# Five tiles instead of two sum the residual and the last expert's product in PSUM, at the end of a hybrid decoder layer

## The reference

```python
out = jnp.zeros_like(t)
for e in range(N_EXPERTS):
    a = t @ p['w_gate'][e]
    u = t @ p['w_up'][e]
    out = out + combine[:, e:e + 1] * ((jax.nn.silu(a) * u) @ p['w_down'][e])
...
x = x + mix @ p['w_out']
x = x + _moe(_rmsnorm(x, p['norm2_g']), p)
...
y = xf * lax.rsqrt(jnp.mean(xf * xf, axis=-1, keepdims=True) + EPS) * g
```

## Time and profile before

| | us |
|---|---|
| median of three runs | 755.19 |
| lowest, highest | 754.53, 789.18 |
| span of the profiled execution, first to last instruction | 752.6 |
| PE busy in it | 664.4 (88%) |
| DVE busy | 273.3 (36%) |
| ACT busy | 161.3 (21%) |

### The profile page before, as it was taken

The page is one execution under the profiler, slowest core; times in us unless marked ns, Lnnn a source line. Parts: engine busy times, 40 slices in busy tenths (PEclk is TensorE's granted clock), DMA queues, the critical chain, the costliest instruction groups (busy, mean ns, idle before and its releaser), DMA issues.

```text
span 752.6 us, 9463 instructions
## 1 busy us (share of the span) xinstructions
PE 664.4 (88%) x3280; PEld 320.5 (43%) x3280; DVE 273.3 (36%) x546; ACT 161.3 (21%) x317; POOL 89.3 (12%) x161
## 2 busy tenths in 40 slices
PE   8999989999998999986999997877787877779995
PEld 4488878863556333332333332322232322223331
DVE  7798995295366221120111111111111111112057
ACT  3677411321613011110111110101001001001033
POOL 5100000000001111211022121112111111111000
PEclk9999999999999999997999999999989999999998
DMA  9523006469556999999999999999999999999993
GB/s 328 202 112 113 1 13 267 177 259 432 190 196 229 363 412 404 409 378 396 425 417 396 402 415 395 420 402 408 410 391 391 422 412 410 402 391 413 425 356 119
DMA packets 29574, 246.55 MB, mean 328 GB/s; under 512 B 6578, under 2 KB 7090, under 8 KB 16592
## 3 DMA queue, kind: packets, MB, share of 16 engines
q1 hardware_dynamic: 22784, 233.95, 77.4%
q0 software_dynamic: 5280, 8.20, 3.3%
q10 hardware_dynamic: 1456, 3.62, 1.3%
HBM read 235.65 MB, written 19.20 MB: 339 GB/s over the span
## 4 chain that ended last, share of the span: by engine, by line
PE 47%; DMA 34%; DVE 11%; ACT 2%; issue 2%; another core or an unknown queue 1%; SPq 1%; POOLq 0%; DVEq 0%
PE psA L1389 25%; PE psB L1389 22%; DMA mem<-in_w_gu 19%; DMA mem<-in_w_down 11%; DVE mem L710 5%; DMA mem<-y_d 2%; DVE mem L934 1%; DMA mem<-in_w_vb 1%; DMA y_d<-mem 1%; ACT front_c L643 1%; DVE mem L849 1%; PE psA L1394 1%; ACT mem L651 1%; DVE mem L861 1%
## 5 line engine op out<-in xcount | busy, mean ns | idle before, releaser
L1389 PE MATMUL psA<-mem 128*64 128x512 f32 (+7 forms) x1348 | 317.4, 535 | 31.7 <-DMA mem<-in_w_gu 15.7
L1389 PE MATMUL psB<-mem 128*64 128x512 f32 (+7 forms) x1210 | 274.0, 552 | 34.7 <-DMA mem<-in_w_gu 17.8
L1389 PEld LDWEIGHTS psA<-mem 128*64 128x64 f32 (+4 forms) x1348 | 145.0, 154 | 184.4 <-issue 142.1
L1389 PEld LDWEIGHTS psB<-mem 128*64 128x64 f32 (+3 forms) x1210 | 110.9, 154 | 178.0 <-issue 132.7
L710 DVE TENSOR_TENSOR mem<-mem 128x512 f32<-128x512 f32 (+17 forms) x116 | 67.3, 595 | 23.8 <-ACT mem L543 19.6
L1307 POOL DMA_INDIRECT y_d<-front_c,mem x30 | 27.5, 916 | 288.8 <-DVE front_c L1114 288.8
L1142 DVE TENSOR_TENSOR front_c<-front_c,psB 64x512 f32<-64x512 f32 x15 | 10.3, 690 | 125.6 <-ACT front_c L643 125.6
L1142 DVE TENSOR_TENSOR front_c<-front_c,psA 64x512 f32<-64x512 f32 x15 | 10.3, 690 | 119.3 <-ACT front_c L643 119.3
L1302 POOL DMA_INDIRECT mem<-hn_d,mem x34 | 33.4, 984 | 92.6 <-DMA hn_d<-front_c 65.0
L643 ACT ACTIVATE front_c<-psA 64x512 f32<-64x512 f32 x15 | 8.8, 588 | 120.3 <-PE psA L1389 120.3
L643 ACT ACTIVATE front_c<-psB 64x512 f32<-64x512 f32 x15 | 8.8, 588 | 120.1 <-PE psB L1389 120.1
(11 more groups left out here) (244 smaller groups left out, 391.4 us busy)
## 6 DMA issues: line engine op xcount, KB each, us to landing
mem<-in_w_gu SPq DMA_DIRECT2D x64, 2048.0 KB, 38.9
mem<-in_w_down SPq DMA_DIRECT2D x32, 2048.0 KB, 44.3
mem<-in_w_out SPq DMA_DIRECT2D x2, 2048.0 KB, 7.9
y_d<-mem SPq DMA_DIRECT2D x1, 4096.0 KB, 11.8
mem<-y_d SPq DMA_DIRECT2D x8, 512.0 KB, 8.4
mem<-in_x_T SPq DMA_DIRECT2D x8, 260.0 KB, 8.6
mem<-in_w_vb SPq DMA_DIRECT2D x8, 256.0 KB, 8.8
mem<-in_x_prompt SPq DMA_DIRECT2D x4, 512.0 KB, 11.1
```

The costliest lines, as they stand in the source:

```text
L1389: return nc.tensor.matmul(out, lhsT, rhs, start=start, stop=stop, skip_group_check=True)
```

## The change

All five tiles are now summed in PSUM. PE multiplies the identity with `x2` for tiles 4, 2 and 3 too, after their `kept`; for the tile of 8 rows the identity is cut to 8 x 8. `add_kept`, its three sums on DVE and the semaphore `f_sum` are gone. ACT waits for `f_ps` in every tile and squares from PSUM. DVE scales all tiles from PSUM. The order of the tiles and their banks stay.

```diff
-        IN_PSUM = (0, 1)
...
             for n, t in enumerate(LAST_ORDER):
                 r = ROWS[t]
-                if t in IN_PSUM:
-                    act.wait_ge(f_ps, n + 1)
-                    total = LAST_PS[t]
-                else:
-                    act.wait_ge(f_sum, n + 1 - len(IN_PSUM))
-                    total = x2[0:r, t, :].rearrange("p (a n) -> p a n", a=2)
-                A(yin[...], total, ACT.Square, accum_out=fx[0:r, t:t + 1]).then_inc(f_sq, 1)
+                act.wait_ge(f_ps, n + 1)
+                A(yin[...], LAST_PS[t], ACT.Square, accum_out=fx[0:r, t:t + 1]).then_inc(f_sq, 1)
...
-            def add_kept(n, t):
-                dve.wait_ge(f_ps, n + 1)
-                dve.wait_ge(f_acc, n + 1)
-                x2t = x2[0:ROWS[t], t, :].rearrange("p (a n) -> p a n", a=2)
-                tt(x2t, x2t, LAST_PS[t], ALU.add).then_inc(f_sum, 1)
...
-            for n in range(2):
-                scaled(n, n)
-            add_kept(2, LAST_ORDER[2])
-            for n in range(3, NT):
-                add_kept(n, LAST_ORDER[n])
-                scaled(n - 1, LAST_ORDER[n - 1])
-            scaled(NT - 1, LAST_ORDER[NT - 1])
+            for n, t in enumerate(LAST_ORDER):
+                scaled(n, t)
...
-            rest(0)
-            pe.wait_ge(y_last, 2)
-            kept(0, 0)
-            rest(1)
-            kept(1, 1)
-            kept(2, LAST_ORDER[2])
-            kept(3, LAST_ORDER[3])
-            pe.wait_ge(f_done, 1)
-            kept(4, LAST_ORDER[4])
+            rest(0, 0, True)
+            pe.wait_ge(y_last, 2)
+            kept(0, False).then_inc(f_ps, 1)
+            rest(1, 1, True)
+            kept(1, False).then_inc(f_ps, 1)
+            for n in (2, 3):
+                kept(LAST_ORDER[n], True)
+                rest(n, LAST_ORDER[n], False).then_inc(f_ps, 1)
+            pe.wait_ge(f_done, 1)
+            kept(LAST_ORDER[4], True)
+            rest(4, LAST_ORDER[4], False).then_inc(f_ps, 1)
```

More of the change, by code:

```diff
@@ L262, in build @@
             sem, "x2_out zero_out tokens_rdy cw3_rdy cw_ps picks_rdy rest_out y_last".split())
-        f_acc, f_ps, f_sum, f_sq, f_rt, f_done, f_out = map(sem, "f_acc f_ps f_sum f_sq f_rt f_done f_out".split())
+        f_acc, f_ps, f_sq, f_rt, f_done, f_out = map(sem, "f_acc f_ps f_sq f_rt f_done f_out".split())
         block = ctx.enter_context(nc.Block())
@@ L686, in _ @@
                 r = ROWS[t]
-                if t in IN_PSUM:
-                    act.wait_ge(f_ps, n + 1)
-                    total = LAST_PS[t]
-                else:
-                    act.wait_ge(f_sum, n + 1 - len(IN_PSUM))
-                    total = x2[0:r, t, :].rearrange("p (a n) -> p a n", a=2)
-                A(yin[0:r, 2 * t, :].rearrange("p (a n) -> p a n", a=2), total, ACT.Square, accum_out=fx[0:r, t:t + 1]).then_inc(f_sq, 1)
+                act.wait_ge(f_ps, n + 1)
+                A(yin[0:r, 2 * t, :].rearrange("p (a n) -> p a n", a=2), LAST_PS[t], ACT.Square, accum_out=fx[0:r, t:t + 1]).then_inc(f_sq, 1)
                 act.wait_ge(f_sq, n + 1)
@@ L1211, in _ @@
                 add_rows(t)
-            def add_kept(n, t):
-                dve.wait_ge(f_ps, n + 1)
-                dve.wait_ge(f_acc, n + 1)
-                x2t = x2[0:ROWS[t], t, :].rearrange("p (a n) -> p a n", a=2)
-                tt(x2t, x2t, LAST_PS[t], ALU.add).then_inc(f_sum, 1)
             def scaled(n, t):
                 r = ROWS[t]
-                total = LAST_PS[t] if t in IN_PSUM else x2[0:r, t, :].rearrange("p (a n) -> p a n", a=2)
                 dve.wait_ge(f_rt, n + 1)
                 link(V.reciprocal(ss[0:r, 3, t:t + 1], ss[0:r, 2, t:t + 1]))
-                V.scalar_tensor_tensor(x2[0:r, t, :].rearrange("p (a n) -> p a n", a=2), total, ss[0:r, 3, t:t + 1],
+                V.scalar_tensor_tensor(x2[0:r, t, :].rearrange("p (a n) -> p a n", a=2), LAST_PS[t], ss[0:r, 3, t:t + 1],
                                        gfb[0:r].rearrange("p (a n) -> p a n", a=2), ALU.mult, ALU.mult).then_inc(f_done, 1)
             dve.wait_ge(rest_in, 16 * 5)
-            for n in range(2):
-                scaled(n, n)
-            add_kept(2, LAST_ORDER[2])
-            for n in range(3, NT):
-                add_kept(n, LAST_ORDER[n])
-                scaled(n - 1, LAST_ORDER[n - 1])
-            scaled(NT - 1, LAST_ORDER[NT - 1])
+            for n, t in enumerate(LAST_ORDER):
+                scaled(n, t)
         @block.gpsimd
@@ L1794, in _, with rest, kept @@
             down(psB[:, 3, :], hT[:, 1], NE - 1).then_inc(dn_ps, 1)
-            def rest(t):
-                pe.wait_ge(f_acc, t + 1)
+            def rest(n, t, first):
+                r = ROWS[t]
+                pe.wait_ge(f_acc, n + 1)
                 for h in range(2):
-                    mm(LAST_PS[t][:, h, :], ident[:, :], x2[:, t, 512 * h:512 * h + 512], True, False)
-            def kept(n, t):
+                    ins = mm(LAST_PS[t][:, h, :], ident[0:r, 0:r], x2[0:r, t, 512 * h:512 * h + 512], first, not first)
+                return ins
+            def kept(t, first):
                 for h in range(2):
-                    if n == 0:
+                    if t == 0:
                         pe.wait_ge(y_last, 3 + h)
-                    ins = mm(LAST_PS[t][:, h, :], picks[:, 128 * t:128 * t + ROWS[t]], yst[:, 1, 512 * h:512 * h + 512], t not in IN_PSUM, True)
-                ins.then_inc(f_ps, 1)
-            rest(0)
+                    ins = mm(LAST_PS[t][:, h, :], picks[:, 128 * t:128 * t + ROWS[t]], yst[:, 1, 512 * h:512 * h + 512], first, not first)
+                return ins
+            rest(0, 0, True)
             pe.wait_ge(y_last, 2)
-            kept(0, 0)
-            rest(1)
-            kept(1, 1)
-            kept(2, LAST_ORDER[2])
-            kept(3, LAST_ORDER[3])
+            kept(0, False).then_inc(f_ps, 1)
[4 more added lines that the diff above has]
+                rest(n, LAST_ORDER[n], False).then_inc(f_ps, 1)
             pe.wait_ge(f_done, 1)
-            kept(4, LAST_ORDER[4])
+            kept(LAST_ORDER[4], True)
+            rest(4, LAST_ORDER[4], False).then_inc(f_ps, 1)
 _NAMES = ['x_prompt', 'x_sample', 'x_T', 'w_xa', 'w_ga', 'w_ub', 'w_vb', 'pack', 'b_T', 'c_T', 'ws_T', 'gmlp_norm_g',
```

## The result

| | before | changed |
|---|---|---|
| median of ten runs, us | 754.46 | 757.14 |
| lowest, highest | 753.24, 789.18 | 755.82, 758.99 |
| profiled span | 752.6 | 754.5 |

The ratio is 1.0039 (95% interval 1.0029 to 1.0049), so the change makes the kernel 2.9 us slower (2.2 to 3.7). The single run of 789.18 us, 4.8% above the fastest for a reason that nothing here shows, is left out of the ratio. The changed kernel's profiled execution took 756.24 us, 1.7 us more than its span. In every later run on record the two differ by 1.7 to 1.9 us; the 2.6 us given ahead of the prediction set the median of the runs against the span of another, faster execution. The prediction, 757.3 us in a range of 753.5 to 760.5, held.

The account below looks back on a forecast made before the run. DVE, started by a landing, was taken to bound the end, with PE becoming last. Added groups 5.25 less PE's spare 1.97 and the last sum's 1.21 give 2.07; 755.19 + 2.07 = 757.3 us, range 753.5 to 760.5.

Parts of the forecast that it names:

- The bound before: End of the old kernel: DVE, started by a landing of table rows, sets it, with PE 2 us ahead.
- The price on PE: Three added groups, `rest` of tiles 4, 2 and 3: 1.81 and twice 1.72 us, 5.25 us (bounds 5.13 and 5.49).
- the rival of the cheap small product: `rest(4)`, with 8 rows in, costs nearly nothing: 1.81 us come off, 755.5 us; chance 0.04.
- Loads uncovered: Added PE groups pay their weight loads, 0.76 us each, 2.28 us in all: 759.5 us; chance 0.05.
- The end behind PE: ACT squares 1.92 us after PE's last group starts, at 748.62; DVE ends 2.99 us later, at 751.61, 2.07 later than before.
- The old wait for `f_done`: PE's wait guarding tile 3's banks: over at 739.88 us, `kept(3)` comes at about 745.0, so it becomes idle.
- The clock: PE's end: clock stays full without a gap; rival of half clock from `rest(0)`, 17.2 us more, 774.5 us, chance 0.01.
- The bound on the gain: DVE alone at the end, three sums removed: ends at 745.5 instead of 749.54, a gain of 4.1 us at best.
- the forecast 2.07: The last tiles: 5.25 us added on PE less 1.97 spare and 1.21 for the removed last sum, 2.07 us slower.
- A late landing in before: Tile 3's rows land later in timed runs than profiled, delaying only the old kernel: 751.1 to 755.2 us; chance 0.10.

Follow-up runs that it names:

- The late landing: Two extra 0.5 MB transfers ahead of tile 3's loads, added to the kernel before (757.38 us) and to the changed kernel (756.28 us).
- The first comparison: The changed kernel against the kernel before: median 757.14 us, ratio 1.0039.
- the second: The changed kernel again, without added transfers, as base of the two kernels with delayed tile 3 loads: 757.4 us, ratio 1.0040 against before.
- the third: The changed kernel a third time, unaltered, against the kernel before: ratio 1.0026.
- The kernel with the old semaphore numbers: The changed kernel with `f_sum` declared again and unused, so later semaphores keep their old numbers, against the kernel before: ratio 1.0024.

## Why the prediction was right

**The bound before.** Right: a landing and DVE behind it. The late landing moves the old kernel's end by 21.27 - 18.84 = 2.43 us and the changed one's by none.

**The price on PE.** 5.25 us for three groups, with 1.81 for the narrow one; the trace has 1.81 + 1.72 + 1.72 = 5.25, and leaving them out gives 5.24. One row did not exist before, 512 columns with 8 rows in and 8 columns of weights. It costs 1.81 us from start to start like its neighbours; the rival of the cheap small product is out. The Trainium skill (TensorE: Matmul & The Clock Gate, "Why this matters for your kernels") says that a single product with 32 rows in takes as long as one with 128. The trace agrees for 8 rows, 588 ns an instruction against 592:

```profile
L1370 PE MATMUL psB<-mem,ident 128*128 128x512 f32 x4 | 1.9, 592 | 0.0
L1370 PE MATMUL psB<-mem,ident 8*8 8x512 f32 x4 | 1.9, 588 | 0.0
```

**Loads uncovered.** Out: the pitch of the added groups is that of the old ones, with weight loads of 0.19 us in each instruction (0.09 in the narrow groups). The rule on row groups of the Trainium skill (TensorE: Matmul & The Clock Gate, "Part 3: Packing small matmuls"), which the prediction set against the change, would have made the three groups 7.5 us by its estimate; the trace disagrees with 5.25.

**The end behind PE.** 1.92 us from the last group's start to ACT's square predicted, 748.52 - 746.61 = 1.91 seen; 2.99 from there to DVE's end predicted, 2.96 seen. DVE's end is 2.02 us later in the measure from `rest(0)`, against 2.07. Behind DVE 754.5 - 751.48 = 3.0 us are left, as before. The old wait for `f_done` is idle, as predicted: `kept(3)` follows at 1.72 us.

**The clock.** PEclk stays at 1.00 to the end of PE's work, in stretches of the changed kernel (length; busy PE, PEld, DVE, ACT, POOL; PEclk, DMA share, GB/s):

```profile
747.00:748.50 1.50, 1.49 (x4) 0.38 (x2) 1.05 (x1) 0.00 (x0) 0.00 (x0) 1.00 0.00 0
748.50:750.00 1.50, 0.00 (x0) 0.00 (x0) 0.00 (x1) 1.41 (x3) 0.00 (x0) 1.00 0.74 303
750.00:752.00 2.00, 0.00 (x0) 0.00 (x0) 1.45 (x2) 0.00 (x0) 0.00 (x0) 0.78 0.09 35
752.00:754.50 2.50, 0.00 (x0) 0.00 (x0) 0.00 (x0) 0.00 (x0) 0.00 (x0) 0.50 0.51 210
```

**What was off.** The bound on the gain, 4.1 us with DVE alone, was too high: without the groups it was 3.2. It took DVE alone and left out that PE's last group, with ACT and DVE behind it, would then set the end. The prediction's own rows give that: 749.54 - (741.45 + 1.92 + 2.99) = 3.18 us. In the three profiles of before the landing was not late. And 757.3 against 757.14 is a closer hit than the working earns: the base of three runs, 755.19, was 0.7 us above the median of ten, 754.46, and the loss in the ratio, 2.9 us (2.2 to 3.7), is 0.9 above the forecast 2.07, which lies just outside its interval. The two misses cancel by luck. What the traces confirm is the 2.0 us at the end.

**What stays open.** The trace accounts for 2.0 us. The first comparison has 2.9 (2.2 to 3.7), the second 3.0 (1.8 to 4.1), the third 2.0 (0.5 to 3.5). The kernel with the old semaphore numbers has 1.8 (0.4 to 3.2). The difference of up to 1 us would lie ahead of `rest(0)`, where the instruction order is the same and where single executions of one kernel differ by more: 729.74 and 732.02 us for the same variant in two profiles. The profiles don't show it there: `rest(0)` starts at 729.55 to 730.99 us in three profiles of before and at 730.20 to 731.45 in four of the changed kernel, which overlap. Chance would explain it; a small effect of the program's layout isn't excluded. A late landing in before was in none of its three profiles, and nothing points to the semaphore numbers.

## What to carry to other kernels

Before moving work off the engine that sets the end, read the spare time of the engine that gets it: the wait between its result and its use (1.97 us here). Once the receiver is the last to finish, the change gains the spare time and the last removed step less the price of the moved work. Here the two together are 1.97 + 1.21 = 3.18 us and a unit costs 1.72: one unit gains 1.5 us, three lose 2.0. For two the same sum gives a loss of about 0.3 us, an estimate that no run tests. Which unit is moved should matter too, since behind the other engine only the last removed step lies on the chain. By estimate, moving tile 2 instead of tile 3 would gain only 1.97 - 1.72 = 0.25 us; that wasn't run either.

## What the runs showed of the hardware

Changes of the weights' shape cost PE about 0.1 us each where a group begins. From 128 x 128 to 128 x 8, to 8 x 8 and back to 128 x 128 the groups start 1.81 us apart, against 1.72 between groups of one shape, whether or not the PSUM tensor changes. The group that returns to 128 x 128 pays 0.1 us once more within itself (1.82 to the next start); its first instruction is 0.70 us long against the usual 0.59, as is `rest(0)`'s, which follows a group with 64 columns of weights (from two narrow windows of the changed kernel's timeline):

```profile
741.35 0.70 PE L1370 MATMUL psB<-front_c 128*128 128x512 f32 x1
...
743.17 0.59 PE L1370 MATMUL psB<-mem,ident 128*128 128x512 f32 x1
```

Beside its 512 columns the rows and the columns of weights of a product do not matter here: 588 to 593 ns an instruction for 8 x 8, 128 x 8 and 128 x 128 within a run of one shape. PEclk is 1.00 up to 750 us, 0.78 on average in 750 to 752 and 0.50, the 1.2 GHz level, after that; PE stopped at 748.5 us, so nothing here waits for it.
